# First projection of a two-block model: no barrier in front, sums of squares moved, bias table stored in sixteen transfers

## The reference

```
hn = _rmsnorm(h, norm_g[i])          # y = x * rsqrt(mean(x*x) + eps) * g
u  = hn @ w_in[i]                    # 2048 -> 5632
a_val, a_glu, a_z, q, k, v, b_z = split(u)
ya = conformer_conv(a_val, a_glu, ...)     # GLU, depthwise conv of width 31, LayerNorm, swish
yb = window_attention(q, k, v, bias_band, sink)   # 16 heads, banded, relative position bias
```

## Time and profile before

| | us |
|---|---|
| median of three runs | 2680.03 |
| profiled execution, its own time | 2679.73 |
| its span in the trace | 2677.6 |
| TensorE busy | 2351.7 |
| VectorE busy | 1690.6 |
| ScalarE busy | 974.6 |
| GpSimd busy | 643.7 |

### The profile page before, as it was taken

One profiled execution on the slowest core, in us unless ns is written; L12 is line 12 of the kernel. 1 busy time (PEld: TensorE's weight loads), 2 busy tenths in 40 slices (PEclk: granted clock), 3 DMA queues, 4 the chain that ended last, 5 costly groups with the idle time before them and its releaser, 6 DMA issues. The chain is left out here.

```text
span 2677.6 us, 48879 instructions
## 1 busy us (share of the span) xinstructions
PE 2351.7 (88%) x19512; PEld 2294.7 (86%) x19512; DVE 1690.6 (63%) x2679; ACT 974.6 (36%) x979; POOL 643.7 (24%) x329
## 2 busy tenths in 40 slices
PE   5999689998999599989978427959999999999997
PEld 4999679998999589979977416849999999999997
DVE  2776548775774568566666575537777776445766
ACT  4333443343334443443323501123444443333333
POOL 2888301226876112410000010002000000331002
PEclk9999869999999699989988858869999999999999
DMA  8555314444554234435533000005455554554554
GB/s 229 173 179 184 128 34 157 173 177 153 188 184 161 67 107 176 173 125 182 180 139 115 32 20 17 2 1 188 171 179 183 188 187 170 179 186 173 188 185 175
DMA packets 70591, 388.86 MB, mean 145 GB/s; under 512 B 15040, under 2 KB 22464, under 8 KB 25584
## 3 DMA queue, kind: packets, MB, share of 16 engines
q1 hardware_dynamic: 68448, 383.59, 40.2%
q10 hardware_dynamic: 2064, 4.19, 1.1%
HBM read 380.42 MB, written 7.34 MB: 145 GB/s over the span
## 5 line engine op out<-in xcount | busy, mean ns | idle before, releaser
L197 ACT ACTIVATE whi<-raw 128x2048 fp32r<-128x2048 f32 x348 | 665.5, 1914 | 930.6 <-DMA raw<-weights_dram 896.4
L215 PE MATMUL ps<-opA,whi 128*128 128x256 f32 x3264 | 924.6, 283 | 33.5 <-PEq L936 14.0
L216 PE MATMUL ps<-opA,whi 128*128 128x256 f32 x3264 | 923.0, 283 | 0.6 <-issue 0.6
L217 PE MATMUL ps<-opA,low 128*128 128x256 f32 x3264 | 923.0, 283 | 0.0
L202 DVE TENSOR_TENSOR low<-raw,whi 128x2048 fp32r<-128x2048 f32 x260 | 596.7, 2295 | 123.9 <-ACT whi L197 95.0
L215 PEld LDWEIGHTS ps<-opA,whi 128*128 128x128 f32 x3264 | 619.2, 190 | 36.0 <-issue 24.8
L216 PEld LDWEIGHTS ps<-opA,whi 128*128 128x128 f32 x3264 | 619.0, 190 | 0.9 <-issue 0.8
L217 PEld LDWEIGHTS ps<-opA,low 128*128 128x128 f32 x3264 | 618.9, 190 | 0.0
L209 POOL TENSOR_TENSOR low<-raw,whi 128x2048 fp32r<-128x2048 f32 x88 | 409.7, 4666 | 181.5 <-ACT whi L197 181.5
L215 PE MATMUL ps<-opB,whi 128*128 128x256 f32 x1472 | 417.6, 284 | 27.6 <-PEq L1614 23.4
L216 PE MATMUL ps<-opB,whi 128*128 128x256 f32 x1472 | 416.6, 283 | 0.0
(11 more groups left out here) (327 smaller groups left out, 2644.0 us busy)
## 6 DMA issues: line engine op xcount, KB each, us to landing
raw<-weights_dram SPq DMA_DIRECT2D x350, 1024.0 KB, 4.8
bias_t<-table_dram SPq DMA_DIRECT2D x16, 384.0 KB, 3.3
table_dram<-tb ACTq DMA_DIRECT2D x1, 4096.0 KB, 45.1
hT<-xT_dram SPq DMA_DIRECT2D x4, 512.0 KB, 10.1
lora_sb<-lora_dram SPq DMA_DIRECT2D x1, 2048.0 KB, 8.0
out_dram<-hT SPq DMA_DIRECT2D x4, 512.0 KB, 2.6
p_in<-pT_dram SPq DMA_DIRECT2D x2, 256.0 KB, 2.8
chunk_mats_dram<-lower SPq DMA_DIRECT2D x4, 128.0 KB, 2.6
```

What stands on the lines that cost most here:

```text
L197: act.activation(whi[:, v % RING, :], raw[:, v % RING, :], ACT.Copy).then_inc(hi_done.sem, 1)
L215: pe.matmul(dst, whi[:, s, w0:w0 + P], op[:, k, 0:T], start=start, stop=False)
L216: pe.matmul(dst, whi[:, s, w0:w0 + P], op[:, k, T:2 * T], start=False, stop=False)
L217: return pe.matmul(dst, wlo(s, w0, w0 + P), op[:, k, 0:T], start=False, stop=stop)
```

## The change

Three things are changed, all of them for the first layer's projection alone:

- The prologue has no block of its own: its engine programs stand at the head of `phase_in`'s block, so each engine goes from one to the other without meeting the rest. Two waits take the place of the barrier. TensorE waits for all 16 blocks of `opA`'s low half (`x_lo`), and GpSimd waits for the first two units' low parts.
- TensorE no longer sums the squares in the prologue. It does unit 0 of the projection, then the 32 matmul passes of `squares_pe`, then units 1 to 3, written out, and from unit 4 on the loop.
- ScalarE no longer issues the store of the bias table. SP issues it as 16 transfers, one for each head: behind the load that follows unit m, for m from 0 to 15, line m of `tb` goes 128 times over to DRAM (256 KB). SP waits for `tb` once, behind the first load. SP's loop for this layer is written out for all 44 units. The wait for the table is for 256 instead of 16.

```diff
-        with nc.Block() as block:
+        x_lo = sig("x_lo")
+
+        def prologue(block):
...
-                act.wait_ge(*table_sb(1))
-                act.dma_start(table, spread(tb[:, :], P)).then_inc(table_out.sem, 16)
...
-                                           ALU.mult, ALU.subtract)
+                                           ALU.mult, ALU.subtract).then_inc(x_lo.sem, 1)
...
                 pe.matmul(ps[0:HEADS, 2, :], rb[:, :], oh[:, :], start=True, stop=True).then_inc(table_mm.sem, 1)
-                squares_pe(pe, sqs[1])
-        sq_in.passed(4)
-        sq_done.passed(1)
-        loaded.passed(112)
-        hi_new.passed(KB)
+        def prologue_passed():
+            sq_done.passed(1)
+            loaded.passed(112)
+            hi_new.passed(KB)
...
-                act.wait_ge(*table_out(16))
+                act.wait_ge(*table_out(16 * HEADS))
...
             with nc.Block() as block:
+                if l == 0:
+                    prologue(block)
+                    prologue_passed()
+
                 @block.sync
                 def _(sp):
-                    units(sp, u0, 44, lambda j, i, m: sp_unit(sp, u0, j, i))
-                    sp.wait_ge(*table_out(16))
+                    if l:
+                        units(sp, u0, 44, lambda j, i, m: sp_unit(sp, u0, j, i))
+                        return
+                    for m in range(44):
+                        sp_unit(sp, u0, m)
+                        if m == 0:
+                            sp.wait_ge(*table_sb(1))
+                        if m < HEADS:
+                            sp.dma_start(table[m:m + 1, :, :], spread(tb[m:m + 1, :], P)).then_inc(table_out.sem, 16)
+                    sp.wait_ge(*table_out(16 * HEADS))
...
                     link = dve_chain.start(v)
+                    if l == 0:
+                        v.wait_ge(*table_sb(1))
                     link(v.memset(a_in[:, :, :], 0.0))
...
-                    units(pe, u0, 36, lambda j, i, m: pe_unit(pe, u0, j, i, op))
+
+                    n0 = 0 if l else 4
+                    if l == 0:
+                        pe.wait_ge(*x_lo(KB))
+                        for m in range(n0):
+                            pe_unit(pe, u0, m, 0, op)
+                            if m == 0:
+                                squares_pe(pe, sqs[1])
+                    units(pe, u0 + n0, 36 - n0, lambda j, i, m: pe_unit(pe, u0 + n0, j, i, op))
...
                 @block.gpsimd
                 def _(pool):
+                    if l == 0:
+                        pool.wait_ge(lo_done.sem, LEAD)
                     units(pool, u0, 44, lambda j, i, m: pool_split(pool, u0, j, i))
+            if l == 0:
+                sq_in.passed(4)
+                x_lo.passed(KB)
```

## The result

The changed kernel takes 2716.24 us (median of 4 runs, 2713.78 to 2722.88) against 2678.35 us for the kernel before, measured again beside it: ratio 1.0141, interval 1.0113 to 1.0169, some 38 us slower. The forecast was 80 us slower (2760), so the direction was right and the size more than twice too large. The profiled execution took 2722.88 us, with a span of 2721.1.

What follows compares the result with a forecast made beforehand. TensorE, busy 2351.7 of 2677.6 us, was taken as the bound. Fifteen steps of 12.3 us on the load queue put unit 20 80.4 us later: 2679.73 + 80.4 = 2760; own range 2740 to 2785, 8 in 10 2710 to 2822.

Steps and rivals of the forecast that it cites:

- Start of unit 0: First projection's start: unit 0 begins at 20.9 instead of 31.29, 10.4 us earlier, and ends at 26.6.
- Squares: Behind unit 0: 32 passes run from 26.6 to 35.8 without a wait; TensorE then waits 3.2 us for unit 2.
- If the table cost nothing: At unit 4 of the first projection: it would run 56.1 to 61.8 against 73.2, 11.4 us gained.
- The price of a row: On SP's queue: one line's 256 KB transfer from one partition takes 9.8 us, bounds 0.9 to 37.5.
- The sum: Units 5 to 20: transfer and load add to 12.3 us a step, fifteen times; unit 20 done at 244.7, 80.4 us later.
- The start of 45.7: On SP's queue: load 5, issued at 42, has its packets end at 45.7, where the fifteen steps begin.
- The signs: Changed profile: table transfers land after 10 to 15 us or more, TensorE idle about half of 56 to 230 us, some 100 GB/s.
- SP is never late: First projection's loads: each is issued some 14 us after its unit's fourth predecessor's data, before its queue turn at 49 us.
- Rival B: First projection: table transfers and loads overlap, only the transfers count, 15 x 9.8 us, 37.5 us less: 2723; chance 0.09.
- Queue order: On SP's queue: each engine takes one ring's descriptors in order, so a load waits behind a table transfer; different issuers' rings alternate.

Runs made afterwards that it cites:

- the early split: Kernel with lines on all 128 partitions, 256 KB transfers, plus ScalarE splitting units 2 and 3 before the square root: 2671.92 us, ratio 0.9972.
- the two kernels whose transfers read more partitions: Changed kernel with 256 KB transfers read from 16 partitions: 2670.98 us, ratio 0.9967; from all 128 partitions: 2676.13 us, ratio 0.9980.
- one row alone: Changed kernel with the one-partition transfer of line 0 issued before the first load, on an idle queue: 2718.75 us, a single execution.
- order and repetition of partitions: Changed kernel with lines sent in order 0, 4, 8, 12, 1 and so on: 2685.64 us, ratio 1.0017; with line m mod 4 each time: 2727.81 us, 1.0183.
- Half a row behind each load: Changed kernel with 64 repeats per one-partition transfer instead of 128, so 32 transfers of 128 KB behind the first 32 loads: 2675.35 us, ratio 0.9982.

## Why the prediction was right or wrong

- *Start of unit 0*: 20.9 forecast, 20.94 measured. It ends later than 26.6 (load 4, which waits for it, is issued at 28.54, not 27.1). Its first matmul lasts 0.58 us, as unit 4's did in the earlier trace rows. TensorE's matmuls and granted clock in stretches of 2 us, two of the changed kernel and one of the kernel before:

```profile
22.00:24.00 2.00, 2.00 (x11) 1.00 0.01 4
26.00:28.00 2.00, 2.00 (x20) 1.00 0.00 0
...
66.00:68.00 2.00, 2.00 (x11) 0.50 0.88 219
```

The unit begins at 11 matmuls in 2 us, which is what the kernel before does at a granted clock of 0.50 (1.2 GHz), and ends at 20, although the rows show 1.00 for both. Before the change the squares ran right ahead of unit 0, and its first matmul lasts 0.36 us. I had overlooked this, 1.4 us. Whether the clock was the lower one here, the rows do not show.

- *Squares*: the sums are ready as forecast (35.8, taken at 35.53), and TensorE waits for unit 2 behind the square root; the early split takes this wait away, as its mechanism says.
- *If the table cost nothing*: 11.4 us gained; 10.1 and 10.6 in the two kernels whose transfers read more partitions.
- *The price of a row*: 9.8 us from the old store's 103 GB/s by four; one row alone went at 26 to 29 GB/s. Right. The Trainium skill's 27.2 GB/s a port, with partitions 0 to 3 on one port and partitions 0 to 15 on four ("SBUF — State Buffer", "Door 1: The DMA port swizzle") agrees with the 27 GB/s and the 103 GB/s, and order and repetition of partitions moved the time as such groups would have it.
- *The sum*: here the step failed. "Then the queue is never empty: row 1, load 6, row 2, load 7 ... fifteen times 9.8 + 2.5 = 12.3 us." The start of 45.7 is 46.0 by its own terms (42 + 4.9 - 0.9), which changes little. Apart from half a microsecond near 52.5 us the queue was never empty, but a step took 9.26 us, and 15 x 3.04 = 46 us is all of the error: unit 20 was forecast at 244.7 and left at 200.63, 44 us earlier. I had taken it that a row and a load never share the engines' time. They do: of row 0 about 80 KB had moved before load 4 landed, and a step on one path is about 10 us, little more than the path's own time. Half a row behind each load shows the same in another size. That an engine's reads run ahead of its writes would explain it; no trace here shows reads and writes apart, so this cause stays open.
- The term is mis-sized twice. Twelve of the fifteen steps average 10.1 us instead of 12.3, 26 us in all. The other three, the short ones, take 17.2 us together instead of 36.9, 20 us in all. At the first two the next row reads another path, at the third the rows end. I read the first two so: engines that are ahead no longer disturb those still at the old row. That partitions 0 to 3 alone have no such steps is shown; the way the engines drift is argued.
- *The signs*: the loads issued from 80 to 180 us landed after 21.6 us in the median, and the DMA engines were busy most of the time, as said. But TensorE was busy 110.36 us of 140, not half, and 153 GB/s moved, not 100. "SP is never late" failed too, see below, and cost nothing that the traces show.
- Rival B named what happens, with a chance of 0.09, and said that it "needs the engines to drift apart by a whole load". It needs less: with 80 KB of a row under the load before it, a step is already near 10 us. Queue order itself was not the point: on a queue of their own the rows held up the loads no less.

## What to carry to other kernels

A DMA that repeats one partition goes at that partition's path, 27 GB/s here, although it is spread over 16 engines, and the loads beside it wait, on the same queue (21.6 us to landing) or on another (21.4). Cut a repeated store across its partitions, not along them; the same 256 KB from 16 partitions left TensorE no wait for a late load. When two transfers of different limits follow one another, bound their sum from below by the longer one alone before adding them.

## What the runs showed that was not expected

- A DMA's issue is not always short. With several transfers still in the queue, SP is held in it: 5.57 us at 63.57 in the changed kernel, against 0.33 for a load's issue at 28.54. Loads behind such an issue go out late: VectorE had taken unit 16 at 163.98, but the load into its buffer was issued at 168.12, as soon as row 15's issue of 5.13 us was over. This costs nothing as long as older transfers fill the queue.
- With the old store in front, a load's packets did not take turns from the start: from 34 to 44 us only the store's queue had packets, though unit 4's load was issued at 37.42. With the store put back in the changed kernel the load is issued 8.5 us earlier (28.95) and unit 4 is split 8.5 us earlier, yet the store still made unit 6 wait. Why the load's packets start so late is not shown.
- Executions of one kernel differ by more than the effects of some edits here (2669.6 to 2692.87 for the kernel before in one comparison), so a gain of 5 us inside the first projection is seen in the trace and not in the median.
